# Where ScalarE's silu stands among its weight splits in the gathered experts of a two-block transformer

## The reference

```python
def moe_swiglu(h, router_w, w1, w3, w2):
    logits = (h @ router_w).astype(F32)
    top_v, top_i = lax.top_k(logits, TOP_K)          # 2 of 8 experts a token
    probs = jax.nn.softmax(top_v, axis=-1)
    gates = jnp.sum(jax.nn.one_hot(top_i, N_EXPERTS, dtype=F32) * probs[..., None], axis=-2)
    ...
    for e in range(N_EXPERTS):
        out = out + gates[..., e:e + 1] * swiglu(h, w1[e], w3[e], w2[e])
```

## Time and profile before

| | |
|---|---|
| median of 3 runs | 2995.88 us |
| lowest, highest | 2987.46, 2998.45 us |
| span of the profiled execution | 2998.3 us (its time is known as this span) |
| TensorE busy | 2809.1 us, 94% |
| TensorE weight loads busy | 2479.9 us, 83% |
| DVE busy | 1916.2 us, 64% |
| ScalarE busy | 1168.2 us, 39% |
| gathered experts | about 985 to 1240 us of the span |

### The profile page before, as it was taken

How to read it: one execution, slowest core, us unless ns; L and a number is a source line. 1 busy time by engine, 2 the same in 40 slices (tenths; PEclk the granted TensorE clock), 3 DMA queues, 4 the chain that set the end, 5 groups by cost and what they waited for, 6 DMA issues and landing times.

```text
span 2998.3 us, 43215 instructions
## 1 busy us (share of the span) xinstructions
PE 2809.1 (94%) x17144; PEld 2479.9 (83%) x17144; DVE 1916.2 (64%) x2619; ACT 1168.2 (39%) x1477; POOL 118.0 (4%) x227
## 2 busy tenths in 40 slices
PE   3889999999999888899999999999999999878999
PEld 3779997899999888888888778888888888654999
DVE  5877679567768766687575356546666466534555
ACT  3445454544444655532224224213242132413543
POOL 0010000000000000000000000000000000000000
PEclk9999999999999999999999999999999999868999
DMA  7677766446667877455452333444434443200455
GB/s 275 218 243 256 263 211 222 145 169 199 232 209 230 300 253 241 165 195 186 138 190 84 105 100 109 156 142 152 167 106 150 144 156 126 71 8 0 165 185 168
DMA packets 116613, 512.10 MB, mean 171 GB/s; under 512 B 12608, under 2 KB 16064, under 8 KB 116304
## 3 DMA queue, kind: packets, MB, share of 16 engines
q1 hardware_dynamic: 81776, 382.12, 37.8%
q0 software_dynamic: 32112, 117.45, 11.8%
q10 hardware_dynamic: 2544, 9.96, 0.9%
HBM read 508.43 MB, written 1.05 MB: 170 GB/s over the span
## 4 chain that ended last, share of the span: by engine, by line
PE 74%; DVE 14%; ACT 5%; issue 4%; DMA 3%; ACTq 0%; DVEq 0%; SPq 0%; POOLq 0%
PE PS L1833 20%; PE PS L1835 20%; PE PS L1834 20%; DVE wlo L967 5%; DMA raw<-in_wstream 2%; ACT whi L525 2%; PE PS L1945 2%; PE PS L1949 2%; PE PS L1946 2%; DVE ada L988 1%; PE PS L1844 1%; DVE ada_first L988 1%; PE PS L2516 1%; DMA ada<-in_adastream 1%; PE PS L2515 1%
## 5 line engine op out<-in xcount | busy, mean ns | idle before, releaser
L525 ACT ACTIVATE whi<-raw 128x1408 fp32r<-128x1408 f32 (+2 forms) x540 | 720.1, 1344 | 872.8 <-PE PS L1835 754.5
L967 DVE TENSOR_TENSOR wlo<-raw,whi 128x1408 fp32r<-128x1408 f32 (+2 forms) x540 | 842.3, 1580 | 253.0 <-ACT whi L525 252.1
L1833 PE MATMUL PS<-h_hi,whi 128*128 128x256 f32 (+1 forms) x2656 | 863.1, 325 | 16.0 <-DVE wlo L967 7.4
L1835 PE MATMUL PS<-h_hi,wlo 128*128 128x256 f32 (+1 forms) x2656 | 858.7, 323 | 0.0
L1834 PE MATMUL PS<-h_lo,whi 128*128 128x256 f32 (+1 forms) x2656 | 855.3, 322 | 0.0
L1833 PEld LDWEIGHTS PS<-h_hi,whi 128*128 128x128 f32 x2656 | 500.1, 188 | 60.2 <-DVE wlo L967 10.0
L1835 PEld LDWEIGHTS PS<-h_hi,wlo 128*128 128x128 f32 x2656 | 500.4, 188 | 43.1
L1834 PEld LDWEIGHTS PS<-h_lo,whi 128*128 128x128 f32 x2656 | 499.2, 188 | 43.7 <-issue 0.2
L1833 PE MATMUL PS<-hid_hi,whi 128*128 128x256 f32 (+1 forms) x1232 | 405.0, 329 | 4.3 <-DVE wlo L967 4.3
L1835 PE MATMUL PS<-hid_hi,wlo 128*128 128x256 f32 (+1 forms) x1232 | 403.8, 328 | 0.0
L1834 PE MATMUL PS<-hid_lo,whi 128*128 128x256 f32 (+1 forms) x1232 | 402.1, 326 | 0.0
(11 more groups left out here) (432 smaller groups left out, 3271.3 us busy)
## 6 DMA issues: line engine op xcount, KB each, us to landing
raw<-in_wstream SPq DMA_DIRECT2D x244, 704.0 KB, 4.7
raw<-in_wstream SPq DMA_DIRECT2D x176, 768.0 KB, 5.0
ada<-in_adastream POOLq DMA_DIRECT2D x222, 512.0 KB, 4.5
raw<-in_wstream SPq DMA_DIRECT2D x120, 512.0 KB, 3.9
ada_first<-in_adastream ACTq DMA_DIRECT2D x6, 1536.0 KB, 22.7
X<-in_xT SPq DMA_DIRECT2D x1, 1024.0 KB, 14.1
X<-in_ctxT SPq DMA_DIRECT2D x1, 1024.0 KB, 5.8
cond<-in_c_rows POOLq DMA_DIRECT2D x1, 1024.0 KB, 5.6
```

The source lines that it names most:

```text
L525: nc.scalar.activation(whi[:, q % SLOTS, 0:n], raw[:, q % SLOTS, 0:n], ACT.Copy).then_inc(hi_split, 1)
L967: nc.vector.tensor_tensor(wlo[:, q % SLOTS, 0:n], raw[:, q % SLOTS, 0:n], whi[:, q % SLOTS, 0:n].bitcast(F32), ALU.subtract).then_inc(lo_s ...
L1833: mm(o, left[0], right[0], start=start, stop=False)
L1835: return mm(o, left[1], right[0], start=False, stop=stop)
```

## The change

In the gathered experts' up half, ScalarE's order is rewritten. Ahead of the wait for group v and its silu, only the panels up to `ceil(moe_end / 12)` are split, those that hold the group's own tiles. The others, up to `moe_end // 12 + 3` as before, follow behind the silu, ahead of `few_high`. The orders of DVE, TensorE, SyncE and GpSimd are the same.

```diff
-                def splits(r, g):
-                    while nxt[0] < moe_ahead(r, g):
+                def splits_to(end):
+                    while nxt[0] < end:
                         split_hi(p0 + nxt[0])
                         nxt[0] += 1
+
+                def splits(r, g):
+                    splits_to(moe_ahead(r, g))
...
                     for v in range(6):
                         n = 2 if v < 5 else 1
-                        splits(r, v)
+                        splits_to(-(-moe_end(r, v) // SLOT))
                         wait_moe_group(act, r, v)
...
+                        splits(r, v)
                         if v:
                             few_high(v - 1)
```

## The result

The changed kernel takes 3053.12 us (median of 4 runs, 3039.72 to 3058.14); the kernel before took 2991.67 us on the same chip (2985.12 to 2998.45, 4 runs). The ratio is 1.0196, with a 95% interval of 1.0172 to 1.022: slower by about 59 us (the two medians lie 61 apart). The profiled execution spans 3055.1 us, against 2998.3.

What follows compares the result with a forecast made beforehand. The prediction took TensorE, busy 94% of 2998.3 us, as the bound. Waits at full clock, +39 us, and falls of the clock, +13, made +52 on the median of 2995.88: 3048 us, range 3023 to 3073.

Steps and rivals of the forecast that it cites:

- The path, 3.80 us: From TensorE's end of a group through silu, high split and low split to its first matmul on the next panel: 3.80 us.
- Lead of 4, 8, 0, 4, 8 tiles: Split weights TensorE still holds at the ends of groups 0 to 4; with the waits, 40.6 us for an expert.
- Expert 2, +11: After group 2, sums wait for DVE's additions to X: 9 us more, and 2 more for half clock.
- Expert 3, +4: DVE's two short instructions and ScalarE's modulations ahead of splits: 0 to 5.3 us, taken as 4.
- Full clock, +39: Four up stretches without falls of the clock: 177.4 us in place of 138.8, so +39 us.
- The clock, 12 falls at 1.1, +13: TensorE's clock falls at eight waits of 3 us and more and half of eight smaller: 12 falls, +13 us.
- The price of a fall: 48 matmuls take 1.70 us longer after a fall; part lies in a wait, so 1.1 us was taken.
- Down halves unchanged: The experts' down halves stay as they are: their splits are not moved and start from the same lead.
- Faster: Rival: the late silu hurts and moved splits would have waited for landings anyway; -12 us, 2984 us, chance 0.06.
- No difference: Rival: the new waits are no longer than the old TensorE waits they replace; chance 0.05.
- No further falls: Rival: the clock stays up or expert 3 costs nothing; +35 to +39, 3031 to 3035 us; few, none or smaller sum 0.22.
- every wait costs the clock: Rival: 20 falls at 1.7 us in the up stretches, +73 us, 3069 us; chance 0.17.

Runs made afterwards that it cites:

- The extra read: Changed kernel, with ScalarE reading the first moved panel once more between silu and high split in groups 0 to 4 of expert 0: 3062.08 us.
- the warmed kernel: Changed kernel, with 16 to 26 unneeded matmuls on TensorE ahead of each of expert 0's five waits for a moved panel: 3040.98 us.

## Why the prediction was right

3053.12 us were measured where 3048 were predicted, within 3023 to 3073. As a difference, +59 us stand against +52: the kernel before came out at 2991.67 here, 4 us under the median to which the prediction added its sum, and that brings the two times closer than the two differences. The mechanism is the predicted one. Step by step:

- **The path, 3.80 us.** Measured 3.89 in the timeline above: 0.20, 0.28, 1.50, 1.76, and 0.15 for the rest, where the prediction had 0.05. The extra read confirms that each microsecond on it counts.
- **Lead of 4, 8, 0, 4, 8 tiles.** At full clock the first expert's groups are 8.85, 8.01, 9.56, 8.68, 6.23 us in the warmed kernel; predicted 8.60, 7.92, 9.29, 8.60, 6.2. Sum 41.3 against 40.6.
- **Expert 2, +11.** By the timeline row below this list, the sums resumed at 1170.11, 9.37 us after the turn behind group 2 (1160.74), 8.98 of it idle; predicted 9.4, where the kernel before was idle for 6.70. The stretch is 53.2 us, with 1.6 for a fall after group 0 (its group 0 to 1 took 10.23, and 8.67 at full clock in the warmed kernel): 51.6, as predicted (40.6 and 11).
- **Expert 3, +4.** At full clock throughout, in the warmed kernel, its stretch is 45.0 us: 3.7 more than the first expert's 41.3. Its groups take 9.59, 8.64, 10.00, 9.91 and 6.90 us, where the first expert has 8.85, 8.01, 9.56, 8.68 and 6.23. Groups 1 to 2 and 4 to the turn are longer by 0.6 and 0.7, as the sum has it for DVE's two short instructions (0.66), and those behind groups 0 and 3, with the modulations, by 0.7 and 1.2, where the sum allowed up to 1.7 each. With the 0.4 of group 2 to 3 this makes the 3.7, where 4 was taken.
- **Full clock, +39.** The stretches' +58.7 less the clock's 18 (below) is between 40 and 41. Experts 0 and 1 are 0.7 longer each than the sum for an expert, expert 3 is 0.4 longer than its own.
- **The clock, 12 falls at 1.1, +13: mis-sized.** The count was nearly right. The granted clock fell behind 16 of the 20 waits. Four of these falls stand at the wait after group 4, where they cost nothing that shows (6.29 against 6.23 us), and one at expert 2's group 2, which the kernel before had too. That leaves 11. The predicted count has a slip in it: beside the nine waits of 3 us and more there are eleven smaller ones, not eight, and half of eleven would make 13 or 14 falls.
- **The price of a fall: the step that failed.** In the first expert it was 1.61 and 1.62 for two falls and 2.90 and 2.40 for two that lasted longer, 8.5 us in all. For the others I compare groups with the same ones at full clock: 10.29, 12.16 and 10.31 in expert 1 (5.8 us), 10.23 in expert 2 (1.6), the whole stretch in expert 3 (2.2 for three falls). Together 18 us for 11 falls, 1.6 to 1.7 each, where the sum had 13. What failed is "part of each lies in a wait, so I take 1.1". It holds in expert 3, 0.4 to 1.0 for a fall: in the warmed kernel TensorE waits there for later low splits too, five times by 0.2 to 0.3 us, and in the kernel after, at the lower clock, all but one of these waits are gone. Whether that is the whole of what hides, no run shows. The step fails in the other three experts: no such wait shows in the first one of the warmed kernel, most falls come just behind the wait, when TensorE is already late, and those that begin well inside a wait last longer. The full 1.70 of the earlier trace rows would have been nearer. The first expert's 8.5 us are shown by an experiment; the rest compares executions, and expert 1's part compares it with other experts.
- **Down halves unchanged.** Expert 1's came out 2 us shorter, in all five kernels that have the changed order there; expert 0's is the same to 1 us. The prediction had given this no term.
- **The rivals.** *Faster* is out: TensorE's waits for `few_lo` did fall from 5.7 to 1.1 us, but those for low splits rose by 35. Its first half was right, though: the late silu did hurt, and the kernel in which only the third panel of group 2 stands behind the silu is 8 us faster than the one before. *No difference* is out with it. *No further falls* and *every wait costs the clock* are both out by the count of 16, and by their sums, 35 to 39 and 73 against 59.

The Trainium skill, "TensorE: Matmul & The Clock Gate", section "HAM oscillation — how this bites in real kernels", describes bursts that each begin at half rate behind a wait for data. The trace after agrees for 16 of the 20 waits, with mean clocks of 0.65 to 0.75 behind those shown in the last section, and not for the three of 1.1 us idle and one of 2.71; expert 3 of the warmed kernel agrees for none of its five.

The row for expert 2, from TensorE's timeline of the kernel after:

```profile
1170.11 0.37 PE L2176 MATMUL PS<-tables,stage_b 128*128 128x1 f32 x1 [8.98 <-DVE X L1506]
```

## What to carry to other kernels

On an engine that works in order, ask of each instruction that waits for the bottleneck engine what stands behind it in the queue: whatever the bottleneck needs next must be ahead of it, on every engine of the chain. Compare the lead with the round trip: here leads of 0 to 1.4 us against 3.8 cost 59 us, and leads of 2.05 to 3.4 us cost nothing that the time shows. Work that isn't needed until a step later may well go behind it, and gained a little here. And if a wait of some microseconds recurs ahead of TensorE, price the fall of the clock behind it at its full length, unless TensorE has further waits behind it that can hide a part.

## What the runs showed of the chip

The clock fell behind shorter waits than I had thought. Windows of the kernel after, in the columns of the earlier trace rows, the first microseconds behind five waits:

```profile
1063.80:1070.64 6.84, 6.84 (x46) 6.84 (x47) 3.62 (x3) 1.05 (x2) 0.00 (x0) 0.75 0.75 231
1074.10:1078.64 4.54, 4.54 (x38) 4.49 (x38) 3.84 (x7) 0.00 (x0) 0.00 (x0) 1.00 0.68 239
1082.33:1090.60 8.27, 8.26 (x48) 8.27 (x49) 5.43 (x8) 1.09 (x2) 0.00 (x0) 0.65 0.83 269
1094.40:1101.00 6.60, 6.60 (x43) 6.60 (x44) 3.95 (x4) 1.17 (x1) 0.00 (x0) 0.74 0.76 239
...
1184.59:1189.50 4.91, 4.91 (x43) 4.91 (x44) 3.95 (x4) 1.70 (x2) 0.00 (x0) 1.00 0.77 252
```

And the timeline rows of TensorE at which they begin, with the idle time before them:

```profile
1063.80 0.39 PE L1837 MATMUL PS<-whi,h_hi 128*128 128x256 f32 x1 [1.99 <-DVE wlo L971]
...
1074.10 0.38 PE L1837 MATMUL PS<-whi,h_hi 128*128 128x256 f32 x1 [1.09 <-DVE wlo L971]
...
1094.40 0.39 PE L1837 MATMUL PS<-whi,h_hi 128*128 128x256 f32 x1 [2.71 <-DVE wlo L971]
...
1184.59 0.38 PE L1837 MATMUL PS<-whi,h_hi 128*128 128x256 f32 x1 [2.71 <-DVE wlo L971]
```

And one for comparison, from expert 3 of the warmed kernel, behind its group 2:

```profile
1233.81 0.36 PE L1837 MATMUL PS<-whi,h_hi 128*128 128x256 f32 x1 [3.51 <-DVE wlo L971]
```

Behind 1.99 us of idle time the clock went from 2.4 to 1.2 GHz for part of the stretch (mean 0.75); behind 1.09 us it stayed. Behind 2.71 us it fell in one place (0.74) and stayed in another (1.00), and in the kernel before it stayed through 2.46. In expert 3 of the warmed kernel it stayed through all five waits, also through the 3.51 us of the last row:

```profile
1233.81:1239.91 6.10, 5.88 (x48) 5.68 (x49) 6.09 (x10) 2.05 (x4) 0.00 (x0) 1.00 0.79 259
```

Fourteen waits of 3.51 us stand in all the traces of this document, and this is the only one without a fall. So in this kernel idle time of about 2 to 3.5 us may or may not cost the clock, and the idle time alone doesn't say which.
